# A block step of the w_mix_out product, first group, computed with seven half-size products in place of eight

## The reference

```python
merged = gc * conv_branch + ga * attn_branch
x = x + jnp.einsum('bsd,de->bse', merged, w_mix_out[l])
h = rmsnorm(x, g_mlp[l])
u = jnp.square(jax.nn.relu(jnp.einsum('bsd,df->bsf', h, w_ff1[l])))
x = x + jnp.einsum('bsf,fd->bsd', u, w_ff2[l])
```

## Time and profile before

| | us |
|---|---|
| median of 3 runs | 2367.91 |
| lowest, highest | 2367.68, 2369.33 |
| the profiled execution, its own time | 2369.1 |
| its span in the trace | 2367.3 |
| PE busy | 2362.3 |
| DVE busy | 1787.1 |
| ACT busy | 1292.2 |

### The profile page before, as it was taken

One profiled execution on the slowest core, in us unless ns is written; L12 is line 12 of the kernel. 1 busy time (PEld: TensorE's weight loads), 2 busy tenths in 40 slices (PEclk: granted clock), 3 DMA queues, 4 the chain that ended last, 5 costly groups with the idle time before them and its releaser, 6 DMA issues.

```text
span 2367.3 us, 31012 instructions
## 1 busy us (share of the span) xinstructions
PE 2362.3 (100%) x12510; PEld 2023.8 (85%) x12510; DVE 1787.1 (75%) x1964; ACT 1292.2 (55%) x1512; POOL 0.2 (0%) x4
## 2 busy tenths in 40 slices
PE   9999999999999999999999999999999999999999
PEld 8888888888888888888888888888888888888887
DVE  5575666666877967967968777888778788897888
ACT  5454454554656555556556566556555555555554
POOL 0000000000000000000000000000000000000000
PEclk9999999999999999999999999999999999999999
DMA  7556556665665675665665555556555655565655
GB/s 253 163 176 200 158 196 193 192 191 171 203 203 171 223 231 171 214 197 184 213 195 190 185 187 169 169 178 198 184 187 186 205 177 188 187 221 187 189 173 183
DMA packets 238044, 452.17 MB, mean 191 GB/s; under 512 B 16570, under 2 KB 20780, under 8 KB 237772
## 3 DMA queue, kind: packets, MB, share of 16 engines
q1 hardware_dynamic: 237147, 449.07, 58.8%
q10 hardware_dynamic: 752, 1.12, 0.1%
HBM read 446.46 MB, written 3.67 MB: 190 GB/s over the span
## 4 chain that ended last, share of the span: by engine, by line
PE 99%; DVE 1%; DMA 0%; ACT 0%; issue 0%; ACTq 0%; DVEq 0%
PE PS L696 42%; PE PS L698 21%; PE PS L729 11%; PE PS L731 11%; PE PS L730 11%; PE PS L658 0%; PE PS L625 0%; PE PS L646 0%; PE PS L635 0%; PE PS L563 0%; DVE WL L1335 0%; DMA VR<-in_g_mix 0%; PE PS L708 0%; PE PS L647 0%; PE PS L626 0%; PE PS L552 0%
## 5 line engine op out<-in xcount | busy, mean ns | idle before, releaser
L1335 DVE TENSOR_TENSOR WL<-RAW,WH 128x1024 fp32r<-128x1024 f32 (+1 forms) x844 | 991.0, 1193 | 431.9 <-ACT WH L856 429.4
L696 PE MATMUL PS<-XHL,WH 128*128 128x512 f32 x3968 | 1248.2, 396 | 0.0
L856 ACT ACTIVATE WH<-RAW 128x1024 fp32r<-128x1024 f32 (+1 forms) x845 | 859.4, 1032 | 659.0 <-PE PS L698 455.1
L698 PEld LDWEIGHTS PS<-XHL,WL 128*128 128x128 f32 x3968 | 745.4, 188 | 176.0
L698 PE MATMUL PS<-XHL,WL 128*128 128x256 f32 x3968 | 779.8, 278 | 0.0
L696 PEld LDWEIGHTS PS<-XHL,WH 128*128 128x128 f32 x3968 | 605.1, 189 | 2.1 <-issue 1.0
L729 PE MATMUL PS<-WH,MHL 128*128 128x512 f32 x915 | 356.9, 390 | 0.0
L731 PE MATMUL PS<-WH,MHL 128*128 128x512 f32 x915 | 356.1, 389 | 0.0
L730 PE MATMUL PS<-WL,MHL 128*128 128x512 f32 x915 | 356.0, 389 | 0.0
L731 PEld LDWEIGHTS PS<-WH,MHL 128*128 128x128 f32 x915 | 171.7, 188 | 35.9
L730 PEld LDWEIGHTS PS<-WL,MHL 128*128 128x128 f32 x915 | 171.8, 188 | 35.1
(11 more groups left out here) (226 smaller groups left out, 1613.8 us busy)
## 6 DMA issues: line engine op xcount, KB each, us to landing
RAW<-in_w_ff SPq DMA_DIRECT2D x256, 512.0 KB, 4.2
RAW<-in_w_in SPq DMA_DIRECT2D x224, 512.0 KB, 3.9
RAW<-in_w_up SPq DMA_DIRECT2D x176, 512.0 KB, 4.5
RAW<-in_w_down SPq DMA_DIRECT2D x88, 512.0 KB, 4.3
RAW<-in_w_mix_out SPq DMA_DIRECT2D x32, 512.0 KB, 4.2
RAW<-in_w_out SPq DMA_DIRECT2D x32, 512.0 KB, 4.2
RAW<-in_w_conv_out SPq DMA_DIRECT2D x16, 512.0 KB, 3.6
RAW<-in_w_attn_out SPq DMA_DIRECT2D x16, 512.0 KB, 4.2
```

The costliest lines, as they stand in the source:

```text
L696: mm(PS[:, b + p.banks[j], :], h[:, k, j * P:(j + 1) * P], x[:, kc, :], start=st, stop=False)
L698: t = mm(PS[:, b + p.banks[j], 0:T], l[:, k, j * P:(j + 1) * P], x[:, kc, 0:T], start=False, stop=en)
L856: act(high, raw, AF.Copy).then_inc(*own.made(hi, i))
L1335: tt(low, raw, high.bitcast(f32), sub).then_inc(*own.made(lo, i))
```

## The change

Place 4 of the first group joins place 5 in the list of seven steps. The order of the pairs stays, and so does the set of pairs for which sums of activations are made (pairs 3 and 5, both already wanted by the second group).

```diff
-          "mix": (((0, 1, 2, 4, 3, 5, 6, 7), (5,)), ((0, 1, 2, 4, 3, 5, 6, 7), (4, 5))),
+          "mix": (((0, 1, 2, 4, 3, 5, 6, 7), (4, 5)), ((0, 1, 2, 4, 3, 5, 6, 7), (4, 5))),
```

## The result

| | before | changed |
|---|---|---|
| median, us | 2367.82 (18 runs) | 2372.36 (18 runs) |
| lowest, highest | 2367.29, 2369.62 | 2371.66, 2373.78 |
| ratio, 95% interval | | 1.0019, 1.0012 to 1.0025 |
| span of the profiled execution | 2367.3 | 2370.7 |

The forecast was 2371.3, range 2367.0 to 2373.0. The measured median lies in the range, 1.1 us above the forecast: slower by 4.5 us, of which 3.4 were worked out and 1.1 were not seen.

What follows compares the result with a forecast made beforehand. PE was taken to bound the kernel, almost never idle. Waits 3.54 plus restarts 0.55 less 0.68 for matmuls gave +3.4 us; profiled 2369.1 became 2372.5, less 1.2 to the median: 2371.3 us, range 2367.0 to 2373.0.

Steps and rivals of the forecast that it cites:

- PE pays everything: Whole span: PE is busy 2362.3 of 2367.3 us, so each matmul less saves its pitch and each new wait costs in full.
- the lead at e8: First entry of place 4, first group: DVE's low part ends at 592.30, PE wants it at 592.74, 0.44 us ahead.
- The three matmuls: Place 4, first group: the seven step removes three matmuls of 0.2267 us each, 0.68 us less.
- The list laid out in time: Places 4 and 5: DVE's new order timed from 591.07; five PE waits 3.54, restarts 0.55, matmuls -0.68, 3.41 us later.
- The rule on DVE: Places 4 and 5: by the skill page six unchained hops would be 0.12 us longer each, loss 4.1 us; trace rows preferred.
- The shift is kept to the end: Behind the group: the 3.4 us loss neither shrinks nor grows, as PE has no later waits and the shared banks' lead holds.
- The rival of late banks: Second group's start: PE waits for line 1739 if a unit lands late, losing 0.9 us, to 2372.2; chance 0.10.
- The banks' lead: Second group's start: line 1739 ends 1.38 us ahead of PE before, and 0.7 us ahead after the change.
- the unit of e20: Weight unit of a first-group entry whose low part precedes the line 1721 sums; forecast to land at 607.6, 5.08 us after issue.
- How much lead would be enough: First entry of place 4: over 3 us for no new wait; a lead equal to all waits would give -0.68 us.
- The clock: Rival, the two seven steps or those behind: idle PE drops from 2.4 to 1.2 GHz, 7 to 9 us, about 2377; chance 0.05.
- The median: Whole kernel: 2371.3 us, from the profiled 2369.1 plus 3.4, less 1.2 for that execution lying above the median; 0.14% slower.

Runs made afterwards that it cites:

- e5: Kernel before with the first group's one seven step at place 4 in place of 5; 2370.79 us, group +2.14 us.
- e2: Changed kernel with the activation sums of pair 3 made one item earlier, beside the last w_attn_out product, in own tiles; 2368.78 us, group +0.32 us against before.
- e13: Kernel before with no seven step in the first group, eight plain steps; 2368.18 us, group +0.68 us.
- e6: Changed kernel plus five PE waits on semaphores long reached, spread over the first products; 2370.85 us.
- e7: e2 plus five PE waits on semaphores long reached; 2367.80 us, group +0.32 us against before.
- e10: Kernel before with two seven steps at places 5 and 6 of the first group, order changed, plus five long reached PE waits; 2375.36 us.
- e3: Kernel before, one seven step at place 5, with the activation sums of pair 3 made one item earlier in own tiles; 2367.47 us.

## Why the prediction was right, and where it was not

- **PE pays everything, and the lead at e8 is 0.44 us.** Right. e5 and e2 set the lead apart from the step: with the same lead one step costs 2.14 us, with a lead of 3.5 us two cost 0.32.
- **The three matmuls, 0.68 us.** Right; e13 measures 0.68.
- **The list laid out in time, five waits 3.54, restarts 0.55.** Right: 3.49, and +3.43 us to place 6 for 3.41.
- **The rule on DVE** of the Trainium skill (page "VectorE: DVE Perf Modes", section "The DRAIN you can't avoid"), by which the loss would have been 4.1 us in the group: as the prediction states it, it does not hold here. The changed kernel again has 1.13 us from t13 to t24 (594.28 to 595.41) and 1.26 us from t24 to the next T13, which waits for it (595.41 to 596.67). The prediction gave that section in part only: the section also says that a next instruction that is not held starts earlier, and with this the 1.13 us agrees. What the rows contradict is that a semaphore between two costs nothing: here it is 0.12 us.
- **"The shift is kept to the end, since PE has no waits behind it that could shrink. Could it grow?"** This is the step that fell short. I looked for growth at the next use of the banks, found a lead of 0.7 us (it was 0.37) and stopped there. 1.1 us came 600 us later, at a take-over of banks by the same mechanism, where a unit landed late because PE's instruction load had moved. Nothing in the sum stood for a change of PE's instruction count, and the prediction gave no reason for leaving it out. e6 and e7 give back 1.0 and 0.9 us with five more instructions. The rival of late banks had the right mechanism and very nearly the right price (0.9 us), in the wrong place.
- **The banks' lead** was missed by 0.3 us: I had put the sums of line 1721 at 4.07 us later than before, and they came 4.44 us later (609.13 + 1.24 against 605.93). The landing of the unit of e20 was not the reason; ACT starts on it at 606.35, 607.6 on the scale of before, as reckoned. DVE goes through the five low parts in front of the sums without a gap, in 5.76 us in both kernels. By the working's own list the first of the five starts at 604.53 and the fifth, at hops of 1.14, at 609.1, where I had put it at 608.7, when its high part is ready.
- **How much lead would be enough** was put too low: "over 3 us", and -0.68 for a lead as large as the sum of the waits (3.54). e2 and e7 had 3.5 us and lost 0.32. The lead that is wanted is the lead that there was, the waits, and the four restarts ahead of the last of them: 0.44 + 3.54 + 0.44 = 4.4 us, an estimate.
- **The clock** did not fall for waits of at most 1.55 us, 3.5 us in all. e10 shows that the rival was real: one idle stretch of 5.0 us was followed by a granted clock of 0.50 and cost 2.45 us more, with the restart in it. That is what the Trainium skill says in "TensorE: Matmul & The Clock Gate", section "HAM oscillation — how this bites in real kernels": idle gaps make the clock fall, and the next matmuls pay.
- **The median.** 2371.3 was forecast from the group alone. With the measured 1.1 us it would have been 2372.4. That 2372.36 lies inside the range is in part luck: the range above 2371.3 stood for the restart, a late entry and late banks in this group, not for an instruction load.

No version tried beats the kernel before; e3 equals it and e7 is 0.3 us behind.

## What to carry to other kernels

Where one engine never waits, the worth of less work on it is read from the lead that its suppliers have at that very place, and not from their share of the span: DVE had a quarter of the span to spare and yet 0.44 us here. Lay the suppliers' new list out from the last row that the change does not touch, with chained and unchained hops from the trace; it gave the loss to 0.02 us. And before the sum is closed, count the instructions: a change of a handful moves the instruction loads of everything behind it, and a place far away with a small lead can lose it (0.24 us here: before, line 1681 ends at 1175.73 and PE takes the banks at 1175.97).

## What was not expected of the hardware

- Where an instruction load of 16 KB started among the weight loads, the unit was there 5.6 to 6.8 us after its issue, always 3.2 us behind the start of the load, in five profiles of five; in the nine others it took 4.8 to 5.4 us. Five instructions more on PE took the load out from among the weights in two of two.
- After an idle stretch of 5.0 us PE's pitch was 0.43 us for 4.4 us; after waits of up to 1.55 us it was at once 0.23 again, but for the first matmul (0.34).
- The idle time that the waits list gives for PE is 0.16 us per wait less than what the wait costs by the pitch (2.7 against 3.5 us for five), and the restart of 0.11 comes on top.
- The profile of before reaches the first group 1.2 to 1.9 us later than the thirteen others (570.95 against 569.0 to 569.7). In it the first small matmuls take 0.24 us apiece in place of 0.13, though the granted clock is given as full there.
